# Softmax sums inverted in one folded reciprocal, and both parts of the mixer's weight chunks made on VectorE

## The chip, the core and the metric

The kernel runs on one core of a Trainium2 chip. The core has TensorE (matrix products, out of two weight buffers), VectorE and ScalarE (elementwise work, both can read the products' memory PSUM), GpSimd (elementwise work on the local memory SBUF alone), SyncE (here only a queue that issues transfers) and 16 DMA engines. Each engine runs its own list of instructions in order, and they meet at semaphores. The metric is the device time of one execution in microseconds; lower is better.

## The reference, cut to what matters

Two layers, each a mixer and a feed-forward part, over 16 meta tokens and 512 tokens of width 1024, in float32. The mixer has three branches of 8 heads: attention with forget decay (FOX), latent attention (MLA) and sliding-window attention (SWA).

```python
for l in range(DEPTH):
    h = mixer_block(h, ...)      # h + (sum of 3 gated branches) @ w_o
    h = conv_ffn(h, ...)         # h + (silu(gate) * val) @ w_down, after a convolution of width 3

# in each branch, for each head:
p = jax.nn.softmax(s, axis=-1)
out = jnp.einsum('bhqk,bkhd->bqhd', p, v)
```

The softmax is made without its division: the product of the exponentials with the values is divided by the exponentials' sums at the end, as a product with the inverted sums.

## The kernel before

**Products in three parts.** Every float32 weight block is split: `wh` is its high part (rounded to the format in which TensorE is fast), `wl` what is left. The activations are split alike (`xh`, `xl`), and a product is `wh*xh + wh*xl + wl*xh`. One block is 128x128 weights against 528 columns in two halves: six matmuls, lines 1357, 1360, 1362 in `gemm`.

**Weight chunks.** A layer has 1080 blocks in the order of `PLAN`: 488 of the mixer, then 64 of `w_o`, 352 of the up projection and 176 of the down projection. Eight blocks are one chunk of 128x1024, 135 chunks a layer. SP loads a chunk into one of two places of `raw` (`load`, line 734). VectorE casts it into `wh` (`high_part`, line 1670), GpSimd subtracts and writes `wl` in four pieces (`chunk_low`, line 817). `wh` and `wl` have three places each. At block 8c of the order, VectorE casts chunk c + 2 and GpSimd makes its low part, and SP loads chunk c + 4, once the low part of chunk c + 2 has let its place go.

**The mixer's order.** `mixer_plan` writes one list of events. Each event has an index, which is a block's number, and a rank; each engine's list is the same events sorted by index and rank, some of them moved by a table `LAG`. Between its blocks TensorE so finds the small products of the attention.

**Jobs.** A job is two heads of one branch: jobs 0 to 3 are FOX, 4 to 7 SWA, 8 to 11 MLA. Job j begins with its scores at block `BEGIN[j]` = 65, 94, 122, 161, 192, 222, 250, 282, 319, 354, 384, 429. Its steps:

- `M`, `MM` (from 25 blocks ahead): scores whose row maxima VectorE takes (lines 1962 and 1940), and `NT`: TensorE transposes the maxima (line 1509) and ScalarE places them as the shift.
- `STM`, `ST`: transposed scores (lines 1540 to 1546), VectorE adds the mask (1972, 1985), ScalarE takes the exponential (1255, 1258 for the meta tokens, 1272, 1274).
- `PVM`, `PV`: the products with the values (1565, 1588), two blocks behind the scores. The sums of the exponentials come from columns of ones in the same products.
- `O`: ScalarE copies heads to `oraw` and sums to `osum` (line 1011). `PVM`'s copies into the same tiles wait until GpSimd has read `oraw` of the job before.
- `recip`: VectorE inverts `osum` in four pieces of 128x132, one a block, from block `BEGIN[j]` + 15 (line 1993). Each head's sum stands 64 times, once in each of its 64 partitions.
- `heads`: VectorE multiplies `oraw` by `osum` (line 1998), four blocks later and lagged by two. `head copy`: ScalarE casts it into `oth`, GpSimd writes `otl` (line 1001). The branch's output blocks `y` take these.

**Norms.** A projected tile is normed through its statistic: TensorE sums squares (line 1376), VectorE adds (1797), ScalarE guesses the root (1028 to 1030), VectorE makes one Newton step (`newton`, 1686 or 1688, then 1691) and multiplies (1887 and others). A query tile `mq` of the latent branch is multiplied with the rotation first (1830, 1832 into `rawt`), and its statistic waits for that.

## Time and profile before

| what | value |
|---|---|
| median of 3 runs | 1982.04 us (1978.26 to 1982.62) |
| span of the profiled execution, first to last instruction | 1979.4 us |
| mean granted clock of TensorE | 0.995 |
| TensorE busy | 1914.7 us, 97% |
| VectorE busy | 1159.0 us, 59% |
| ScalarE busy | 766.2 us, 39% |
| GpSimd busy | 1025.5 us, 52% |
| DMA traffic | 156.30 MB, mean 79 GB/s |

The profiled execution has no time of its own beside its span. The span is 1979.4 us and the runs' median 1982.04 us, so some 2.6 us lie around it.

A matmul's end is modelled and overlaps its neighbours, so busy TensorE time does not say how fast it is, but a wait of TensorE shows as idle time with what released it. The first layer's mixer lies at 0 to 545 us, the second's at 1000 to 1540 us; `w_o` and the feed-forward part follow each.

### The profile page before, as it was taken

The numbers are of one execution on the slowest core, as the hardware profiler recorded it, in microseconds if no ns is written. First come the engines' busy times: TensorE is split into PE (matmuls) and PEld (weight loads), VectorE is DVE, ScalarE is ACT, GpSimd is POOL, SyncE is SP. The second block draws the span as 40 slices with busy tenths as digits, with TensorE's granted clock in tenths as the row PEclk, the third lists the DMA queues.
The fourth block names the chain that finished last, engine by engine and source line by source line (L and its number), as shares of the span: only waits on it lengthen the run. The fifth ranks groups of instructions, "written<-read, shape, count | busy, mean of one in ns | idle before, by whom it ended". The sixth has DMA issues, their size and how long they took to land.

```text
span 1979.4 us, 36478 instructions
## 1 busy us (share of the span) xinstructions
PE 1914.7 (97%) x14396; PEld 1817.1 (92%) x14396; DVE 1159.0 (59%) x2121; ACT 766.2 (39%) x1514; POOL 1025.5 (52%) x1306
## 2 busy tenths in 40 slices
PE   7899999999999999999998999999999999999999
PEld 7889998888999999999997899988889999999887
DVE  7665476787465666552256654767874655665411
ACT  5455666655223222220044556666553232222100
POOL 7655454544364444544477455544443645445553
PEclk9999999999999999999999999999999999999999
DMA  4212121211232322332332121112112423323332
GB/s 149 75 44 65 54 65 44 63 45 55 65 129 85 97 86 86 97 93 93 93 109 76 43 65 54 63 46 65 45 53 65 141 86 97 97 86 96 96 97 96
DMA packets 44802, 156.30 MB, mean 79 GB/s; under 512 B 5012, under 2 KB 5268, under 8 KB 44504
## 3 DMA queue, kind: packets, MB, share of 16 engines
q1 hardware_dynamic: 44488, 153.75, 24.7%
q8 instruction: 114, 1.87, 0.4%
q14 instruction: 56, 0.46, 0.1%
q10 hardware_dynamic: 144, 0.22, 0.0%
HBM read 149.63 MB, written 4.26 MB: 78 GB/s over the span
## 4 chain that ended last, share of the span: by engine, by line
PE 77%; DVE 12%; ACT 4%; issue 3%; POOL 2%; DMA 1%; SPq 0%; DVEq 0%; ACTq 0%; POOLq 0%
PE ps L1357 20%; PE ps L1360 19%; PE ps L1362 19%; PE ps L1588 5%; PE ps L1372 2%; PE ps L1368 2%; PE ps L1371 2%; PE ps L1376 2%; DVE osum L1993 1%; DVE rstd L1691 1%; PE ps L1540 1%; PE ps L1501 1%; POOL wl L817 1%; DVE ps L1962 1%; DVE square L1686 1%
## 5 line engine op out<-in xcount | busy, mean ns | idle before, releaser
L817 POOL TENSOR_TENSOR wl<-raw,wh 128x256 fp32r<-128x256 f32 x1076 | 798.7, 773 | 746.5 <-DVE wh L1670 739.9
L1357 PE MATMUL ps<-xh,wh 128*128 128x264 f32 (+1 forms) x2880 | 810.7, 303 | 12.5 <-DVE wl L1750 9.4
L1360 PE MATMUL ps<-xl,wh 128*128 128x264 f32 (+1 forms) x2880 | 764.3, 286 | 0.0
L1362 PE MATMUL ps<-xh,wl 128*128 128x264 f32 (+1 forms) x2880 | 585.4, 285 | 0.0
L1357 PEld LDWEIGHTS ps<-xh,wh 128*128 128x128 f32 x2880 | 546.7, 190 | 31.1 <-issue 18.3
L1360 PEld LDWEIGHTS ps<-xl,wh 128*128 128x128 f32 x2880 | 547.4, 190 | 17.0 <-issue 8.9
L1362 PEld LDWEIGHTS ps<-xh,wl 128*128 128x128 f32 x2880 | 451.2, 190 | 0.0
L1670 DVE CAST wh<-raw 128x1024 fp32r<-128x1024 f32 x270 | 206.6, 765 | 176.0 <-PE ps L1357 89.1
L1588 PE MATMUL ps<-pt,vx 128*128 128x512 f32 (+7 forms) x480 | 157.8, 409 | 3.9 <-ACT pt L1274 2.3
L1985 DVE TENSOR_TENSOR ps<-ps,cst 128x128 f32<-128x128 f32 (+6 forms) x240 | 74.8, 313 | 145.3 <-PE ps L1546 111.0
L1274 ACT ACTIVATE pt<-ps 128x256 f32<-128x256 f32 (+5 forms) x224 | 78.5, 363 | 112.5 <-DVE ps L1985 111.2
L1324 ACT ACTIVATE cv<-ps,prm 128x528 f32<-128x528 f32 (+1 forms) x44 | 34.6, 786 | 209.0 <-DVE ps L2039 209.0
L1357 PE MATMUL ps<-oth,wh 128*128 128x264 f32 (+1 forms) x384 | 111.5, 312 | 2.1 <-ACT ssum L1011 1.7
L2039 DVE TENSOR_TENSOR ps<-ps,rstd 128x528 f32<-128x528 f32 (+1 forms) x88 | 62.1, 706 | 80.5 <-PE ps L1362 80.4
L1360 PE MATMUL ps<-otl,wh 128*128 128x264 f32 (+1 forms) x384 | 100.9, 283 | 0.0
L1993 DVE RECIPROCAL osum<-osum 128x132 f32<-128x132 f32 x96 | 90.0, 958 | 13.2 <-ACT oraw L1011 13.0
L1360 PE MATMUL ps<-al,wh 128*128 128x264 f32 x352 | 93.1, 285 | 0.0
L1357 PE MATMUL ps<-ah,wh 128*128 128x264 f32 x352 | 93.0, 284 | 0.0
L1540 PE MATMUL ps<-xq,xk 97*17 97x16 f32 (+15 forms) x288 | 78.2, 290 | 8.8 <-ACT ptm L1255 4.0
L1501 PE MATMUL ps<-xk,xq 96*128 96x400 f32 (+13 forms) x256 | 71.6, 300 | 9.1 <-DVE nm L1962 3.0
L1588 PEld LDWEIGHTS ps<-pt,vx 128*128 128x128 f32 x480 | 74.6, 191 | 6.2 <-ACT pt L1274 4.1
L1001 POOL TENSOR_TENSOR otl<-oraw,oth 128x528 fp32r<-128x528 f32 x24 | 34.5, 1437 | 87.5 <-ACT oth L1011 86.7
(194 smaller groups left out, 3440.9 us busy)
## 6 DMA issues: line engine op xcount, KB each, us to landing
raw<-weights SPq DMA_DIRECT2D x270, 512.0 KB, 3.5
h<-tokens SPq DMA_DIRECT2D x4, 528.0 KB, 6.9
h<-tokens SPq DMA_DIRECT2D x8, 264.0 KB, 6.0
residual<-h SPq DMA_DIRECT2D x8, 264.0 KB, 5.0
h<-residual SPq DMA_DIRECT2D x8, 264.0 KB, 5.9
out<-h SPq DMA_DIRECT2D x8, 256.0 KB, 4.7
cst<-constants SPq DMA_DIRECT2D x1, 1048.0 KB
extra<-positions SPq DMA_DIRECT2D x18, 4.1 KB
```

Of the source, the lines that this page charges most:

```text
L817: ins = nc.gpsimd.tensor_tensor(wl[c % SPLIT][:, part], raw[:, c % RAW, part], wh[c % SPLIT][:, part].bitcast(F32), ALU.subtract)
L1274: ins = nc.scalar.activation(pt[0:nk, i, 0:nq], bank[0:nk, 0:nq], ACT.Exp)
L1357: a = nc.tensor.matmul(out, a_hi, x_hi[:, sl], start=first, stop=False)
L1360: nc.tensor.matmul(out, a_hi, x_lo[:, sl], start=False, stop=False)
L1362: ins = nc.tensor.matmul(out, a_lo, x_hi[:, sl], start=False, stop=last)
L1501: ins = nc.tensor.matmul(bank[:, col:col + nk], xq[rows, i, e, q], xk[rows, i, e, k0:k0 + nk], start=True, stop=True)
L1540: nc.tensor.matmul(out, xk[rows, i, e, keys], xq[rows, i, e, q], start=True, stop=False)
L1588: ins = nc.tensor.matmul(heads_out[:, c:c + nq], vals, pt[:, i, 0:nq], start=t == 0, stop=t == 4)
L1670: nc.vector.tensor_copy(wh[c % SPLIT][:, :], raw[:, c % RAW, :]).then_inc(s_hi, 1)
L1985: nc.vector.tensor_tensor(sc, sc, cst[0:nk, a:a + n], ALU.add).then_inc(scores_masked.sem, scores_masked.tick((l, j, e, t)))
L1993: nc.vector.reciprocal(osum[:, a:a + T // 4], osum[:, a:a + T // 4]).then_inc(dve_step.sem, dve_step.tick((l, "recip", j, q)))
L2039: nc.vector.tensor_tensor(src[:, skip:T], src[:, skip:T], rstd[:, skip:T], ALU.mult).then_inc(up_scaled.sem, up_scaled.tick((l, t)))
```

## The change

Part one, the inverted sums. In every job but 11 the four `recip` steps and their pieces are replaced:

- `fold` (block `BEGIN[j]` + 15): SP copies the two heads' sums, 2 x 528 numbers, out of one partition each, into 32 partitions of 33 (in rows 96 to 127 of the tile `krr`, two places taken in turn).
- `recip` (3 blocks later): VectorE inverts these 32x33 numbers in one instruction.
- `unfold` (same index): SP stores them to a tensor `inverse` in HBM; `spread` (7 blocks behind `fold`): SP loads each head's 528 inverted sums into its 64 partitions of `osum`, once the store is done.
- `heads` and `head copy` come 9 blocks later than before (`FOLD[2] - 4`).

Part two, the weight chunks. For the chunks of the mixer, from the fourth chunk of the program on, VectorE makes both parts: `high_part` as before, then `low_part`, one subtraction of 128x1024 right behind it. GpSimd makes none of them. For the feed-forward part nothing changes. The rest of the diff gives each part and engine a semaphore of its own, and code for sharing the work that these settings leave unused.

```diff
+FOLD = [3, 7, 13]
+FOLD_N = 2 * T // (P - MQ)
+UNFOLDED = [11]
...
-        for q in range(4):
-            put(i + q, 6, "recip", j, q)
+        if folded(j):
+            put(i, 2, "fold", j)
+            put(i + FOLD[0], 6, "recip", j, 0)
+            put(i + FOLD[0], 7, "unfold", j)
+            put(i + FOLD[1], 8, "spread", j)
+            i += FOLD[2] - 4
+        else:
...
+HIGH_AT = {"dve": 0, "act": 0, "pool": 0}
+LOW_AT = {"dve": 0, "pool": 0}
+POOL_PIECE = 256
+FIRST = 3
+MIX_HIGH, FFN_HIGH = "dve", "dve"
+MIX_DVE, FFN_DVE = 1024, 0
...
+def low_by(c):
+
+    d = CW if c == 0 else 0 if c < FIRST else MIX_DVE if in_mixer(c) else FFN_DVE
+    return {"dve": (0, d), "pool": (d, CW)}
...
             def load(n):
...
-                    sp.wait_ge(s_lo, n - RAW + 1)
+                    for sem, value in low_done(n - RAW):
+                        sp.wait_ge(sem, value)
...
+                    elif s[0] == "fold":
+                        j = s[1]
+                        sp.wait_ge(heads_copied.sem, heads_copied.at(l, j, 1))
+                        sp.wait_ge(meta_heads_copied.sem, meta_heads_copied.at(l, j))
+                        half_rows = (P - MQ) // 2
+                        for e in range(2):
+                            a = e * half_rows
+                            sp.dma_start(fold(j)[a:a + half_rows, :],
+                                         osum[e * HD:e * HD + 1, :].rearrange("o (r c) -> o r c", c=FOLD_N)).then_inc(
+                                sums_folded.sem, sums_folded.tick((l, j), 16))
+                    elif s[0] == "unfold":
+                        j = s[1]
+                        sp.wait_ge(dve_step.sem, dve_step.at(l, "recip", j, 0))
+                        sp.dma_start(inverse[l, j, :, :].rearrange("e (r c) -> (e r) c", c=FOLD_N), fold(j)).then_inc(
+                            inverse_stored.sem, inverse_stored.tick((l, j), 16))
+                    elif s[0] == "spread":
+                        j = s[1]
+                        sp.wait_ge(inverse_stored.sem, inverse_stored.at(l, j))
+                        for e in range(2):
+                            sp.dma_start(osum[e * HD:(e + 1) * HD, :],
+                                         inverse[l, j, e:e + 1, :].broadcast_to([HD, T])).then_inc(
+                                inverse_spread.sem, inverse_spread.tick((l, j), 16))
...
+            def low_part(c):
                 if c >= CHUNKS:
                     return
...
+                a, b = low_by(c)["dve"]
+                if b <= a:
+                    return
+                dve.wait_ge(*high_done(c))
+                nc.vector.tensor_tensor(wl[c % SPLIT][:, a:b], raw[:, c % RAW, a:b], wh[c % SPLIT][:, a:b].bitcast(F32),
+                                        ALU.subtract).then_inc(chunk_low["dve"].sem, chunk_low["dve"].tick((c,)))
...
                         j, q = s[1], s[2]
+                        if folded(j):
+                            dve.wait_ge(sums_folded.sem, sums_folded.at(l, j))
+                            nc.vector.reciprocal(fold(j), fold(j)).then_inc(
+                                dve_step.sem, dve_step.tick((l, "recip", j, 0)))
+                            continue
...
                         j = s[1]
-                        dve.wait_ge(dve_step.sem, dve_step.at(l, "recip", j, 3))
+                        if folded(j):
+                            dve.wait_ge(inverse_spread.sem, inverse_spread.at(l, j))
+                        else:
+                            dve.wait_ge(dve_step.sem, dve_step.at(l, "recip", j, 3))
                         nc.vector.tensor_tensor(oraw[:, :], oraw[:, :], osum[:, :], ALU.mult).then_inc(
                             heads_ready.sem, heads_ready.tick((l, j)))
```

VectorE's list of the kernel before, behind the scores of job 0: the row maxima of job 1 (`ISA` into `nm...`), the reciprocals of job 0, a chunk's CAST at block 80 (the first reciprocal stands right ahead of it).

```order
L1670 CAST wh_52<-raw 128x1024 [waits chunk_started,chunk_loaded0]
L1993 RECIPROCAL osum<-osum 128x132
L1797 SCALAR_TENSOR_TENSOR ssum<-teps,ps 128x528 [waits tile_scaled_down,statistic_ready]
L1962 ISA ps,nmx<-ps,cst 128x400 [waits scores_for_max]
L1962 ISA nmx 128x1
L1993 RECIPROCAL osum<-osum 128x132 x2
L1962 ISA ps,nmx<-ps,cst 128x272 [waits scores_for_max]
L1962 ISA nmx 128x1
L1686 TENSOR_TENSOR square<-ssum,square 128x528 [waits rsqrt_guess_ready]
L1691 SCALAR_TENSOR_TENSOR rstd<-square,rstd 128x528 [waits dve_step]
L1887 SCALAR_TENSOR_TENSOR q_87<-rawt,gain,rstd 128x528 [waits key_doubled,key_low_part,tile_normed]
L1998 TENSOR_TENSOR oraw<-oraw,osum 128x528 [waits dve_step]
```

The same place in the changed kernel:

```order
L1818 CAST wh_52<-raw 128x1024 [waits chunk_started,chunk_loaded0]
L1828 TENSOR_TENSOR wl_55<-raw,wh_52 128x1024 [waits chunk_high_part_by_dve]
L1955 SCALAR_TENSOR_TENSOR ssum<-teps,ps 128x528 [waits tile_scaled_down,statistic_ready]
L2120 ISA ps,nmx<-ps,cst 128x400 [waits scores_for_max]
L2120 ISA nmx 128x1
L2149 RECIPROCAL krr<-krr 32x33 [waits sums_folded]
L2120 ISA ps,nmx<-ps,cst 128x272 [waits scores_for_max]
L2120 ISA nmx 128x1
L1847 TENSOR_TENSOR square<-ssum,square 128x528 [waits rsqrt_guess_ready]
L1852 SCALAR_TENSOR_TENSOR rstd<-square,rstd 128x528 [waits dve_step]
L2045 SCALAR_TENSOR_TENSOR q_87<-rawt,gain,rstd 128x528 [waits key_doubled,key_low_part,tile_normed]
```

Four reciprocals and the product of the heads (`oraw`) are gone from here, one short reciprocal of `krr` and the subtraction into `wl` have come.

ScalarE's list of the kernel before, ahead of the scores of job 6, from the Newton guess to the shift's copies; `oth` is the high part of job 5's heads.

```order
L1028 ACTIVATE square<-ssum 128x528 [waits statistic_taken,tile_scaled_down]
L1029 ACTIVATE rstd<-square 128x528 [waits act_step]
L1030 ACTIVATE square<-rstd 128x528 [waits act_step]
L1011 ACTIVATE oth<-oraw 128x528 [waits heads_ready]
L1011 ACTIVATE xq<-ps 1x384 [waits shift_transposed]
L1011 ACTIVATE xq<-ps 1x128
```

In the changed kernel the same instruction stands between the exponentials of job 6:

```order
L1391 ACTIVATE ptm<-ps,prm 17x16 [waits meta_product_done,meta_scores_masked]
L1391 ACTIVATE ptm<-ps,prm 17x16
L1408 ACTIVATE pt<-ps,prm 128x512 [waits product_done,scores_masked]
L1410 ACTIVATE pt<-ps 128x256 [waits product_done,scores_masked]
L1129 ACTIVATE oth<-oraw 128x528 [waits heads_ready]
L1410 ACTIVATE pt<-ps 128x256 [waits product_done,scores_masked]
L1129 ACTIVATE oraw<-ps 64x16 [waits heads_low_part,meta_product_done]
L1129 ACTIVATE osum<-ps 64x16
```

`oth` now follows the second exponential (`pt`) of job 6. Behind the third stand the meta copies into `oraw` and `osum`, which wait for GpSimd's `otl` (`heads_low_part`).

## Rows read from the trace of the kernel before

**Rows 1.** Windows of the two mixers: stretch, length, busy us (instructions) of each engine, clock, DMA.
```profile
60.00:545.00 485.00, 464.68 (x3386) 429.46 (x3386) 315.12 (x696) 269.40 (x587) 242.82 (x284) 0.99 0.18 56
1060.00:1540.00 480.00, 459.23 (x3403) 424.47 (x3402) 311.30 (x678) 267.20 (x582) 243.25 (x285) 1.00 0.19 58
```
**Rows 2.** Waits of TensorE: who for whom, us in total, times, longest us.
```profile
PE ps L1376 <- DVE rawt L1832: 8.5, 9, 1.1
PE ps L1509 <- DVE nm L1940: 4.7, 5, 2.1
...
PE ps L1540 <- ACT ptm L1255: 4.0, 2, 2.0
```
**Rows 3.** Groups of the page: count, busy us, mean ns, idle before them.
```profile
L817 POOL TENSOR_TENSOR wl<-raw,wh 128x256 fp32r<-128x256 f32 x1076 | 798.7, 773 | 746.5 <-DVE wh L1670 739.9
...
L1670 DVE CAST wh<-raw 128x1024 fp32r<-128x1024 f32 x270 | 206.6, 765 | 176.0 <-PE ps L1357 89.1
...
L1993 DVE RECIPROCAL osum<-osum 128x132 f32<-128x132 f32 x96 | 90.0, 958 | 13.2 <-ACT oraw L1011 13.0
```
**Rows 4.** Timeline of VectorE ahead of job 1's shift: start us, us, what.
```profile
100.17 0.97 DVE L1993 RECIPROCAL osum<-osum 128x132 f32<-128x132 f32 x1
...
104.05 1.81 DVE L1993 RECIPROCAL osum<-osum 128x132 f32<-128x132 f32 x2
...
109.34 0.70 DVE L1998 TENSOR_TENSOR oraw<-oraw,osum 128x528 f32<-128x528 f32 x1
```
**Rows 5.** Timeline of TensorE at four waits, in brackets the idle time and its releaser.
```profile
111.22 0.33 PE L1509 MATMUL ps<-cst,nm 128*128 128x128 f32 x1 [2.08 <-DVE nm L1940]
...
299.95 0.39 PE L1540 MATMUL ps<-xq,xk 97*128 97x256 f32 x1 [1.97 <-ACT ptm L1255]
...
335.62 1.13 PE L1376 MATMUL ps<-sq,cst 96*128 96x264 f32 x4 [0.98 <-DVE rawt L1832]
...
460.69 1.13 PE L1376 MATMUL ps<-sq,cst 96*128 96x264 f32 x4 [1.08 <-DVE rawt L1832]
```
**Rows 6.** Timeline of VectorE ahead of the last three of these waits.
```profile
286.50 1.80 DVE L1993 RECIPROCAL osum<-osum 128x132 f32<-128x132 f32 x2
...
293.93 1.73 DVE L1691 SCALAR_TENSOR_TENSOR rstd<-square,rstd 128x528 f32<-128x528 f32 x1
...
333.34 0.68 DVE L1670 CAST wh<-raw 128x1024 fp32r<-128x1024 f32 x1
...
455.34 1.81 DVE L1993 RECIPROCAL osum<-osum 128x132 f32<-128x132 f32 x2
```
**Rows 7.** Line 1691, the Newton step: duration ns min/median/max.
```profile
L1691 DVE SCALAR_TENSOR_TENSOR rstd<-square,rstd x56: 707/709/1733, 35.0 to 1611.1; 128x528 f32<-128x528 f32 x56
```
**Rows 8.** Windows around three falls of the clock, columns as in rows 1.
```profile
110.00:120.00 10.00, 8.79 (x59) 8.59 (x60) 3.73 (x13) 7.54 (x20) 8.35 (x10) 0.83 0.00 1
296.00:310.00 14.00, 11.87 (x63) 10.11 (x62) 3.96 (x9) 9.27 (x22) 7.12 (x9) 0.76 0.15 46
...
1100.00:1110.00 10.00, 7.93 (x54) 7.55 (x53) 4.56 (x14) 6.49 (x17) 7.15 (x8) 0.83 0.01 2
```
**Rows 9.** Line 1750, VectorE's subtraction for the first chunk, columns as in rows 7.
```profile
L1750 DVE TENSOR_TENSOR wl<-raw,wh x1: 1226/1226/1226, 8.0 to 8.0; 128x1024 fp32r<-128x1024 f32 x1
```
**Rows 10.** Timeline of GpSimd beside the Newton step at 293.93.
```profile
293.48 1.62 POOL L1001 TENSOR_TENSOR otl<-oraw,oth 128x528 fp32r<-128x528 f32 x1
```
**Rows 11.** Chain that ended last, start of layer 1: start us, us, what.
```profile
1031.29 4.98 POOL wl L817 x4
```
**Rows 12.** Timeline of VectorE, start of layer 1.
```profile
1062.01 1.43 DVE L1670 CAST wh<-raw 128x1024 fp32r<-128x1024 f32 x1 [2.76 <-DMA raw<-weights]
```
**Rows 13.** Timeline of ScalarE, the second exponential of job 1.
```profile
118.96 0.51 ACT L1274 ACTIVATE pt<-ps 128x400 f32<-128x400 f32 x1 [0.54 <-DVE ps L1985]
```
**Rows 14.** Timeline of TensorE, the product that takes it.
```profile
121.79 0.83 PE L1588 MATMUL ps<-pt,vx 128*128 128x400 f32 x2
```
**Rows 15.** DMA issues: count, KB each, median us to landing.
```profile
raw<-weights SPq DMA_DIRECT2D x270, 512.0 KB, 3.5
```

## What I expected

> **What bounds the kernel now.** I read the windows of each engine's busy time first, because they split the span by stage. In the mixers TensorE is busy 464.68 of 485 us and 459.23 of 480 us [rows 1]; the feed-forward stages between them are not changed. So TensorE bounds the kernel, and a change to VectorE can give back only TensorE's waits in the mixers: 20 us a layer, and what the clock loses beside them. Next come the waits of TensorE, longest in total first [rows 2]: for the turned query tiles (`L1376` on rawt, nine times), for a job's maxima (`L1509`, where two of the five waits are of 2.1 us), and for the meta probabilities (`L1540` on `L1255`, two of 2.0 us). No row there has TensorE wait for GpSimd's low weight parts, so that these come sooner is worth nothing by itself. Then the costliest groups of the page [rows 3]: 1076 low parts on GpSimd (798.7 us), 270 CASTs on VectorE, 96 reciprocals of 0.96 us. Last, the timelines of the engines around each long wait of TensorE [rows 5, 6].
>
> **Reciprocals.** Each of 24 jobs has 4 x 0.958 us on VectorE [rows 3]. In 22 jobs one takes their place, of 33 elements a partition where each now has 132; by length it takes a quarter, 0.24 us. VectorE saves 22 x (3.83 - 0.24) = 79 us. What that is worth shows at two places, where the reciprocals stand in an unbroken run of VectorE's work that TensorE waits for.
> - At the transposed maxima of job 1 VectorE works almost without a pause from the first reciprocal at 100.17 to the last maximum, and TensorE, whose transpose begins at 111.22, waits 2.08 us for it [rows 4, 5]. In this run go four reciprocals (3.83) and the product at 109.34 (0.70); a subtraction (1.23) and the short reciprocal (0.24) come: 3.06 us less, more than the wait. Two layers: -4.2 us by the 2.1 of [rows 2].
> - At the start of job 6 TensorE waits 1.97 us for the meta probabilities [rows 5]. Before it VectorE has reciprocals (two of them, 1.80 us, at 286.50), then a Newton step of 1.73 us at 293.93 [rows 6] that takes 0.71 elsewhere [rows 7]. Four reciprocals go, less a subtraction at block 240: 2.4 us, more than the wait. Two layers: -4.0 us.
>
> **Clock.** Behind these waits the granted clock falls to the lower of its levels (1.2 of 2.4 GHz) for a while: 0.83 over 10 us, 0.76 over 14 us, 0.83 over 10 us [rows 8]. That is 10 x 0.17 + 14 x 0.24 + 10 x 0.17 = 6.8 us. If the waits go, it should stay up. But a wait that grows past 2 us (below) may bring new falls; I take -4.8, between 0 and -6.8.
>
> **Low parts on VectorE.** Blocks 0 to 487 of a layer are 61 chunks; less the first three of the program, 119 chunks get a subtraction of 128x1024 on VectorE. The one that is there now takes 1.226 us [rows 9]: +146 us. With the reciprocals VectorE has 67 us more on 626 busy of 965 [rows 1], about 72%. GpSimd loses 119 x 4 x 0.77 = 368 us in the mixers. That helps VectorE: the Newton step `L1691` runs from 0.707 to 1.733 us [rows 7], and the one of 1.73 has a head part of GpSimd beside it (1.62 us from 293.48) [rows 10]. Such slowing also touches the CAST (1.43 us at 1062.01, the mean is 0.765) [rows 3, 12]. The Trainium skill (GPSIMD Engine Reference, 1. Specifications) says that GpSimd's SBUF interfaces are shared with VectorE and contend with instructions of two SBUF inputs; the trace agrees with it. The same rule speaks against the change, as the subtraction has two SBUF inputs itself: GpSimd keeps some 118 us of work in 965, so 12% of the subtractions would be about 1 us longer, 14 us of VectorE's time, a tenth of which may reach TensorE; by the rule the sum is 1 us less of a gain, by the row of 1.226 alone it is as below.
>
> Where does 1.23 us at a chunk's start reach TensorE? CAST and subtraction follow each other, 1.9 us in one piece, and what stands behind them waits.
> - Query tiles. The second mq tile of a layer has its CAST at 333.34 right ahead of its two products, and TensorE already waits 0.98 us for these [rows 6, 5]: +1.23. One more mq tile stands so, three blocks ahead of its statistic; for the others reciprocals go just before (the last tile: 1.81 us of them at 455.34, a wait of 1.08 us [rows 6, 5], which I count as gone in both layers, -2). Cost: at most 4 x 1.23 = 4.9; I take +4.
> - Scores. 18 chunk starts a layer fall into the score phases, between mask, exponential and product. In the forget and window jobs there is room: the exponential that ended at 119.47 is used at 121.79, 2.3 us later [rows 13, 14]. The 7 chunk starts a layer in the four latent jobs are tight, as VectorE norms keys there: at most 14 x 1.23 = 17 us, at least 0. I take a quarter of that, nearest to the row with room: +4.
> - Other waits that stand behind reciprocals, under 1 us each: -1.
> - Start of layer 1. The chain of waits runs through GpSimd's low parts there (4.98 us for one chunk at 1031.29) [rows 11], and VectorE waits 2.76 us for a weight load that they hold back [rows 12]. Both go, and the CAST behind is 0.7 longer than the mean: at most 3.5 us; VectorE gets its subtractions in exchange. I take -2. Start of layer 0: three CASTs in VectorE's unbroken run get a subtraction, 3.7 at most, shorter neighbours in exchange: +1.
>
> **Transfers and the later heads.** Per folded job SP issues two small loads, a store and two spreads; the chunk loads behind them in SP's order are needed 16 blocks later, so this costs nothing unless SP stands for over 8 us. The trace prints no landing for a small transfer; 0 and the 3.5 us of a 512 KB load [rows 15] bound it. The new reciprocal stands where the fourth stood, which begins 4.8 us behind the first (the row at 104.05 holds two) [rows 4]; without three of them (2.9) and with a subtraction (1.23) 3.1 us are left. So VectorE waits at most 0.4 us a job there, 9 us in all, mostly off TensorE's path. The product of the heads moves 9 blocks later and in jobs 0, 1, 4, 5 and 9 lands among the next job's scores. Behind it ScalarE's copy, GpSimd's 1.62 us [rows 10] and ScalarE's meta copies follow. In the 2.3 us of room this mostly fits: +1 for both.
>
> **Sum:** -4.2 - 4.0 - 4.8 - 2 - 1 - 2 = -18; +4 + 4 + 1 + 1 = +10; together -8 us. The span of 1979.4 us lies 2.6 us under the median of the runs, 1982.04, and its ends are not changed. Forecast: 1974 us.
>
> **Rivals.**
> 1. VectorE is too full at chunk starts: the tight terms take their upper bounds (scores +17, query tiles +5), the clock falls again behind the grown waits (clock term 0), and the rest stays: -4.2 - 4.0 - 2 - 1 - 2 + 22 + 2 = +11, 1993 us. It decides from the point where more than half of the 14 latent chunk starts show in TensorE's waits. For it: VectorE is at 72% and works in order, its masks are on the shortest loop. Against it: the room of 2.3 us [rows 13, 14], and GpSimd's slowing of VectorE goes.
> 2. The late heads: ScalarE stands at the copy behind the product (0.70), copies (about 0.65), then stands at the meta copies for GpSimd's 1.62, 3.0 us in all. Ten places x (3.0 - 2.3) is 7 us with the room, 30 us without: 1981 to 2004, taken as 1983. For it: they stand between two exponentials in ScalarE's order. Against: the room.
> 3. The transfers are slower than the chunk load bounds them, as two in series behind a load of weights: 7 us instead of 3.5 puts VectorE to wait 3.9 us x 22 = 86 us, as long as the reciprocals were. Then only GpSimd's relief is left, and the subtractions cost what they cost: 1983 us. The Trainium skill (DMA: Bandwidth & Descriptors, Anatomy of one DMA) has about 2.0 us fixed for one DMA on GpSimd's path; by it the fold fits in the 3.1 us, and this rival falls. No row here shows a small landing.
> 4. Larger gain: nearly all of the mixers' waits behind VectorE go, and the clock stays up: the 18, 2 more from the clock, and a third (10) of the 30 us that are left of the 41 of gaps [rows 1], less costs of 5: -25, 1957 us. For it: GpSimd's relief speeds every Newton chain, which I gave no term of its own.
>
> **Chances.** Forecast 0.52 (own range 1966 to 1980), rival 4 0.18, rival 1 0.13, rival 2 0.09, rival 3 0.08. What can be told from no change is 0.2%, 4 us: 1978 to 1986. The forecast's own range is below 1978 in five parts of six: 0.44, rival 4 gives 0.18, rivals 2 and 3 0.04: faster 0.66. Same: 0.08 of the forecast, 0.01 of rival 1, 0.04 and 0.05 of 2 and 3: 0.18. Slower: 0.12 of rival 1, 0.04 of 2 and 3: 0.16. Range 1960 to 1986.
>
> **What would show it.** Right: the waits of 2.1 us at `nm` and 2.0 us at `ptm` are gone, and the granted clock is 1.00 in those stretches; the wait at the second mq tile is about 2.2 us; GpSimd is busy some 370 us less, VectorE some 40 to 70 us more; the CAST's mean is near 0.69 us. Wrong: waits of the products for exponentials in the latent jobs over 8 us in all (rival 1), of ScalarE for GpSimd's head parts that TensorE's waits repeat (rival 2), of VectorE at the folded reciprocal over 1 us each (rival 3). The feed-forward windows must stay as they are; if they move, the sum was made on the wrong stage.

## The result, and the profile after

The changed kernel takes 2019.96 us (median of 4 runs, 2018.09 to 2021.79) against 1981.61 us before (4 runs, 1978.26 to 1982.62). The ratio is 1.0198, 95% interval 1.0184 to 1.0213: 38 us slower. I had forecast 1974 us and a range of 1960 to 1986; the result lies far outside it, on the other side of no change. Every time here is of fast executions: one of the four of run e1 took 3072 us at a mean granted clock of 0.557 and is left out.

Windows of the profiled execution after, by stage (stretch, length, busy us and instructions of each engine, clock, DMA):

```profile
60.00:553.00 493.00, 459.94 (x3302) 421.56 (x3301) 334.57 (x707) 265.12 (x581) 98.35 (x77) 0.99 0.20 60
553.00:1018.00 465.00, 464.93 (x3805) 464.54 (x3804) 242.32 (x339) 97.27 (x140) 214.40 (x298) 1.00 0.30 95
1080.00:1580.00 500.00, 469.01 (x3427) 430.93 (x3427) 340.25 (x700) 267.92 (x582) 97.29 (x77) 0.99 0.20 61
```

Beside [rows 1]: the feed-forward stage is full as it was. In the mixers TensorE now misses 33 and 31 us of these stretches, where it missed 20 and 21. GpSimd is relieved as meant (98 us for 243). The first product of `w_o` starts at 588.1 us instead of 569.6, and the last one of layer 1's `w_o` 36.9 us late: 18.5 us are lost in each mixer. The loss is not spread evenly: TensorE's statistic product (`L1376` before, `L1524` after) that began at 206.84 us begins at 206.62 now, so nothing is lost up to there; the one of 311.88 comes 2.9 us late, the one of 477.87 17.9 us late. Most of it falls into the part where the latent branch's tiles are made and its jobs run.

The waits of TensorE after, beside [rows 2] (for whom: us in total, times, longest):

```profile
PE ps L1524 <- DVE rawt L1990: 16.2, 10, 3.2
...
PE ps L1649 <- DVE nma L2120: 7.0, 4, 3.4
PE ps L1657 <- DVE nm L2098: 6.8, 7, 1.8
PE ps L1649 <- DVE nmx L2120: 4.7, 10, 1.0
...
PE ps L1688 <- ACT ptm L1391: 4.4, 6, 1.4
```

The query tiles' wait (`L1524`, before `L1376`) has doubled from 8.5 us. The maxima's waits (`nm`, `nma`, `nmx` at `L1649`, before `L1501`, and `L1657`, before `L1509`) have grown in number; the waits of 2.1 and 2.0 us that I meant to remove are no longer the longest of their kind, but many others are there.

The groups and transfers that answer to [rows 3, 9, 15], and the Newton step of [rows 7]:

```profile
L933 POOL TENSOR_TENSOR wl<-raw,wh 128x256 fp32r<-128x256 f32 x600 | 434.5, 756 | 453.6 <-DVE wh L1818 453.1
...
L1818 DVE CAST wh<-raw 128x1024 fp32r<-128x1024 f32 x270 | 204.1, 756 | 178.6 <-PE ps L1505 101.1
L1828 DVE TENSOR_TENSOR wl<-raw,wh 128x1024 fp32r<-128x1024 f32 x120 | 171.7, 1431 | 4.1
...
L1828 DVE TENSOR_TENSOR wl<-raw,wh x120: 1224/1226/2295, 8.0 to 1578.4; 128x1024 fp32r<-128x1024 f32 x120
...
osum<-inverse SPq DMA_DIRECT2D x44, 132.0 KB, 2.9
```

```profile
L1852 DVE SCALAR_TENSOR_TENSOR rstd<-square,rstd x56: 707/708/711, 35.5 to 1648.1; 128x528 f32<-128x528 f32 x56
```

The Newton step is never slowed now (1.733 us at worst before). But the subtraction, which I took at 1.226 us, has a mean of 1.431: most take 1.226, and 31 of the 120 take 1.52 to 2.30, each with a GpSimd instruction beside it. The CAST, which I expected at a mean of 0.69 us, has 0.756 (0.765 before).

At the two waits that were to go, and at the last query tile (the two of 1.97 us and 1.08 us in [rows 5] are the second and the third here), TensorE has now:

```profile
112.36 0.33 PE L1657 MATMUL ps<-cst,nm 128*128 128x128 f32 x1 [0.38 <-DVE nm L2098]
...
303.92 0.39 PE L1688 MATMUL ps<-xq,xk 97*128 97x256 f32 x1 [1.27 <-ACT ptm L1391]
...
477.73 1.13 PE L1524 MATMUL ps<-sq,cst 96*128 96x264 f32 x4 [3.23 <-DVE rawt L1990]
```

Ahead of the last of them VectorE stood for the fold's transfer, with the query tile's products behind:

```profile
475.77 0.36 DVE L2149 RECIPROCAL krr<-krr 32x33 f32<-32x33 f32 x1 [3.13 <-DMA krr<-osum]
```

The clock, 1.00 around the same product before (453 to 473 us there), falls behind this wait (columns of the windows above):

```profile
470.00:490.00 20.00, 16.77 (x122) 16.12 (x120) 15.91 (x34) 10.82 (x19) 3.98 (x3) 0.91 0.22 67
```

The loss to the subtractions shows best at the second query tile of the latent branch. VectorE's timeline there, then GpSimd's, then TensorE's:

```profile
336.33 0.68 DVE L1818 CAST wh<-raw 128x1024 fp32r<-128x1024 f32 x1
337.04 2.29 DVE L1828 TENSOR_TENSOR wl<-raw,wh 128x1024 fp32r<-128x1024 f32 x1
339.36 0.71 DVE L1988 TENSOR_TENSOR rawt<-ps,gq 32x528 f32<-32x528 f32 x1
340.08 0.70 DVE L1990 TENSOR_TENSOR rawt<-ps,gq 96x528 f32<-96x528 f32 x1
```

```profile
336.92 1.33 POOL L1101 TENSOR_TENSOR yq<-q,xq 96x528 fp32r<-96x528 f32 x1 [11.50 <-ACT xq L1129]
```

```profile
340.93 1.13 PE L1524 MATMUL ps<-sq,cst 96*128 96x264 f32 x4 [2.92 <-DVE rawt L1990]
```

Before, this wait was 0.98 us [rows 5]. The tile is ready ahead of this CAST (its last weight product begins at 335.60 us and takes 0.41); its first two products on VectorE stand behind 3.0 us of weight work, 1.06 us of which is what this subtraction takes over its usual 1.226, with GpSimd at work beside it.

The maxima of job 0 stand behind a chunk's start in the same way. VectorE, then TensorE:

```profile
62.46 1.23 DVE L1828 TENSOR_TENSOR wl<-raw,wh 128x1024 fp32r<-128x1024 f32 x1
63.60 0.70 DVE L1955 SCALAR_TENSOR_TENSOR ssum<-teps,ps 128x528 f32<-128x528 f32 x1
64.22 0.43 DVE L2120 CUSTOM_DVE_ANT_0 ps<-ps,cst 128x264 f32<-128x264 f32 x1
```

```profile
64.76 0.39 PE L1649 MATMUL ps<-xk,xq 66*128 66x272 f32 x1 [3.02 <-DVE nma L2120]
```

In k1 below, where nothing but the subtractions and SP's order differs, TensorE waits 1.47 us there.

### The profile page after: what moved, and what is told of

It reads as the page before. It is cut to its first block, busy times and chain, and to the rows that moved or that the text cites. A ratio compares the mean times of both kernels' runs of the same rounds, so it can differ in the third digit from the quotient of the medians.

```text
span 2016.3 us, 36044 instructions
## 1 busy us (share of the span) xinstructions
PE 1925.9 (96%) x14396; PEld 1821.9 (90%) x14396; DVE 1226.9 (61%) x2174; ACT 767.9 (38%) x1514; POOL 687.5 (34%) x830
## 3 DMA queue, kind: packets, MB, share of 16 engines
q8 instruction: 114, 1.87, 0.4%
## 4 chain that ended last, share of the span: by engine, by line
PE 73%; DVE 15%; issue 5%; ACT 5%; DMA 1%; SPq 0%; POOL 0%; DVEq 0%; ACTq 0%
PE ps L1505 19%; PE ps L1508 19%; PE ps L1510 18%; PE ps L1736 5%; DVE wh L1818 3%; DVE wl L1828 2%; PE ps L1520 2%; PE ps L1516 2%; PE ps L1519 2%; PE ps L1524 2%; PE ps L1649 1%; DVE rstd L1852 1%; PE ps L1688 1%; DVE ps L2143 1%; ACT square L1146 1%
## 5 line engine op out<-in xcount | busy, mean ns | idle before, releaser
L933 POOL TENSOR_TENSOR wl<-raw,wh 128x256 fp32r<-128x256 f32 x600 | 434.5, 756 | 453.6 <-DVE wh L1818 453.1
L1828 DVE TENSOR_TENSOR wl<-raw,wh 128x1024 fp32r<-128x1024 f32 x120 | 171.7, 1431 | 4.1
L1061 POOL TENSOR_TENSOR yq<-q,xq 64x528 fp32r<-64x528 f32 x32 | 51.6, 1613 | 172.0 <-ACT xq L1129 169.4
L1119 POOL TENSOR_TENSOR otl<-oraw,oth 128x528 fp32r<-128x528 f32 x24 | 36.9, 1537 | 177.7 <-ACT oth L1129 177.7
L1649 PE MATMUL ps<-xk,xq 96*128 96x400 f32 (+13 forms) x256 | 73.6, 308 | 19.0 <-DVE nma L2120 7.0
```

What stands on the lines that cost most here:

```text
L933: ins = nc.gpsimd.tensor_tensor(wl[c % SPLIT][:, part], raw[:, c % RAW, part], wh[c % SPLIT][:, part].bitcast(F32), ALU.subtract)
L1649: ins = nc.tensor.matmul(bank[:, col:col + nk], xq[rows, i, e, q], xk[rows, i, e, k0:k0 + nk], start=True, stop=True)
L1828: nc.vector.tensor_tensor(wl[c % SPLIT][:, a:b], raw[:, c % RAW, a:b], wh[c % SPLIT][:, a:b].bitcast(F32), ALU.subtract).then_inc(chunk_lo ...
```

## The experiments

All times are medians, each ratio is to the kernel before in the same group of runs, with its 95% interval.

| run | fold | low parts | chunk loads by SP | us | ratio |
|---|---|---|---|---|---|
| changed kernel | yes | VectorE, block 0 | block 0 | 2019.96 | 1.0198 [1.0184, 1.0213] |
| e1 | yes | GpSimd | block 0 | 1995.05 | 1.0072 [1.0055, 1.0089] |
| e2 | no | VectorE, block 0 | block 0 | 2054.39 | 1.0365 [1.0340, 1.0391] |
| e4 | yes | VectorE, block 3 | block 0 | 1995.16 | 1.0068 [1.0053, 1.0083] |
| e5 | yes | VectorE, quarters in blocks 0 to 3 | block 0 | 2033.51 | 1.0266 [1.0247, 1.0285] |
| f1 | yes, reciprocal 2 later | GpSimd | block 0 | 2014.12 | 1.0166 [1.0152, 1.0179] |
| f2 | no, heads 9 later | GpSimd | block 0 | 1983.05 | 1.0012 [1.0003, 1.0020] |
| f3 | as f1 | VectorE, block 3 | block 0 | 2011.95 | 1.0154 [1.0140, 1.0168] |
| f4 | as f1 | VectorE, block 5 | block 0 | 2089.29 | 1.0545 [1.0526, 1.0564] |
| f5 | no | VectorE, block 3 | block 0 | 2008.23 | 1.0142 [1.0126, 1.0157] |
| h1 | yes | GpSimd | block 5 | 1978.23 | 0.9989 [0.9980, 0.9998] |
| h2 | yes | VectorE, block 3 | block 5 | 1987.85 | 1.0032 [1.0019, 1.0045] |
| h4 | no | GpSimd | block 5 | 1986.62 | 1.0026 [1.0015, 1.0037] |
| k1 | yes | GpSimd | 5, from block 72 | 1971.51 | 0.9950 [0.9937, 0.9962] |
| k2 | yes | VectorE, block 3 | 5, from block 72 | 1974.64 | 0.9959 [0.9947, 0.9972] |
| k3 | yes | VectorE, block 0 | 5, from block 72 | 2013.42 | 1.0159 [1.0145, 1.0173] |
| k4 | yes, heads 3 sooner | GpSimd | 5, from block 72 | 1966.65 | 0.9926 [0.9912, 0.9939] |
| l1 | yes | VectorE, block 3, CAST too | 5, from block 72 | 1994.77 | 1.0072 [1.0059, 1.0084] |
| l2 | as k4 | VectorE, block 3 | 5, from block 72 | 1966.42 | 0.9924 [0.9911, 0.9938] |

"Block n" is the place within a chunk of eight blocks. All diffs are against the changed kernel.

### The two parts apart: e1, e2

```diff
-MIX_DVE, FFN_DVE = 1024, 0
+MIX_DVE, FFN_DVE = 0, 0
```

> Part one alone: the sums are inverted folded, and GpSimd makes the mixer's low weight parts as before. Theory (the loss of 38 us is in part two, in VectorE's longer piece of work at each chunk's start): near the kernel before or a little under it, 1970 to 1984 us, and the wait of 2.1 us ahead of job 1's shift is gone. Rival (the later heads and their transfers cost it): 2000 us or more.

```diff
-UNFOLDED = [11]
+UNFOLDED = list(range(12))
```

> Part two alone: all 24 jobs keep their four reciprocals and the place of their heads, VectorE makes both weight parts. Theory (loss in part two): at least as slow as the changed kernel, 2018 to 2045 us, as the 79 us of reciprocals stand in the same queue of VectorE. Rival (the loss is in the fold and the late heads): under 1995 us.

Neither reading held whole: e1 lies between its two ranges and e2 9 us above the theory's. Part two is the larger loss: alone +73 us, on top of the fold +25 (1.0198 to 1.0072). But part one alone is not the gain that I had forecast either: +14 us. VectorE's waits for transfers in e1, and its timeline at the last query tile:

```profile
DVE krr L2149 <- DMA krr<-osum: 31.6, 12, 4.8
DVE oraw L2164 <- DMA osum<-inverse: 17.4, 7, 4.3
```

```profile
461.80 0.36 DVE L2149 RECIPROCAL krr<-krr 32x33 f32<-32x33 f32 x1 [3.29 <-DMA krr<-osum]
462.19 0.71 DVE L1988 TENSOR_TENSOR rawt<-ps,gq 32x528 f32<-32x528 f32 x1
```

and of GpSimd and of SP's queue ahead of it:

```profile
455.02 2.83 POOL L933 TENSOR_TENSOR wl<-raw,wh 128x256 fp32r<-128x256 f32 x4 [7.60 <-DVE wh L1818]
```

```profile
447.45 10.75 SPq L814 DMA_DIRECT2D raw<-weights  x2
458.30 1.18 SPq L845 DMA_DIRECT2D krr<-osum  x2
```

ScalarE had copied the sums and heads by 454.3. SP stood in front of a chunk load until GpSimd's low part was done at 457.85, issued 512 KB of weights, and only then the fold, at 458.30. It landed 3.5 us later; VectorE stood 3.29 us for it with the query tile behind, and TensorE 3.38 us at 463.76.

### The low part elsewhere in the chunk: e4, e5

```diff
-LOW_AT = {"dve": 0, "pool": 0}
+LOW_AT = {"dve": 3, "pool": 0}
```

> The changed kernel, but VectorE makes the low part three blocks (some 5.4 us) behind the CAST, so that its work at a chunk's start is two shorter pieces. Theory (the long unbroken piece of 1.9 to 3 us delays what stands behind it): a third to two thirds of the loss comes back, 1994 to 2008 us. Rival (VectorE has too much work in all, wherever it stands): within 5 us of 2020. Second rival (what hurts is which single step stands behind it, not the length): as much is lost at other steps, 2010 to 2025.

```diff
+DVE_PIECES = 4
...
-                if n % BLK == LOW_AT["dve"]:
-                    low_part(n // BLK + AHEAD)
+                if n % BLK < DVE_PIECES:
+                    low_part(n // BLK + AHEAD, n % BLK)
```

> The changed kernel, but VectorE makes the low part in four pieces of 128x256, one a block at blocks 0 to 3 of the chunk; total work of VectorE grows by some 0.06 us a piece. Theory (length of the piece): most of the loss comes back, 1985 to 2000 us, since no step is delayed by more than 0.3 to 0.6 us. Rival (total work): 2020 us or a few us more.

e4 gives 25 us back, as expected; with GpSimd making the low parts (e1) it is no less. e5 was meant to do more and is 13 us slower than the changed kernel. A piece is dearer than I took it for:

```profile
L1831 DVE TENSOR_TENSOR wl<-raw,wh x477: 402/420/1575, 8.0 to 1595.3; 128x256 fp32r<-128x256 f32 x158, 128x1024 fp32r<-128x1024 f32 x1
```

Four pieces of 0.42 us are 1.68 us where one of 1.226 did, and beside GpSimd they reach 1.58 us each. The group took 249.1 us instead of 171.7. A second thing differs: VectorE stood 44.6 us for the fold's transfers where it stood 14.9 in the changed kernel; but in e4 it stood 41.4 us for them. How the 13 us divide was not measured. e5 changed the amount of work and says nothing about the length of a piece; l1 below does.

### More room for the reciprocal, later heads: f1, f2, f3, f4

```diff
-FOLD = [3, 7, 13]
+FOLD = [5, 8, 13]
```

f1 (with GpSimd's low parts):

> Part one alone again (GpSimd makes the low parts), but the folded reciprocal comes five blocks behind the fold instead of three, and the spread eight instead of seven; the heads stay where part one has them. In the run of part one alone VectorE stood 31.6 us, 12 times, up to 4.8 us, for the sums' transfer, and the last query tile stood behind one such wait. Theory (that wait is what makes part one slower than the kernel before): VectorE's wait for krr falls under 10 us in all, TensorE's wait at the last query tile falls from 3.5 to about 1.2 us, and the time to 1982 to 1990 us. Rival (the late heads cost it): 1992 to 1998 us as before.

f2 (no fold, no low parts on VectorE):

```diff
             for q in range(4):
                 put(i + q, 6, "recip", j, q)
+            if j != 11:
+                i += FOLD[2] - 4
```

> No fold and no low parts on VectorE: the kernel before with one thing changed, the product of the heads and ScalarE's copy behind it come nine blocks later in every job but 11. Theory (late heads cost little, the transfers' wait costs): 1979 to 1986 us. Rival (late heads): 1990 us or more.

f3 and f4 (f1's `FOLD`, and `LOW_AT` of VectorE at 3 and at 5):

> Both parts, low part three blocks behind the CAST (1995 us without more) and the folded reciprocal five blocks behind the fold. Theory: the two repairs add up, as they touch different waits: 1980 to 1990 us. Rival (VectorE at this load has no room left for either): 1992 us or more.

> As the run before, but the low part five blocks behind the CAST, one block past the middle of a chunk. Theory (length of the unbroken piece): within 4 us of the run with three blocks. Rival (it is a matter of which single steps stand behind it, as all events of a query tile end at fixed blocks of the plan): differs by over 6 us, in either direction.

The rival in f2 falls: late heads alone cost 2.4 us. My repair in f1 made part one 19 us slower instead of faster. VectorE's waits in f1, and SP's queue and VectorE at job 7's heads:

```profile
DVE oraw L2164 <- DMA osum<-inverse: 47.4, 18, 5.9
...
DVE krr L2149 <- DMA krr<-osum: 1.9, 3, 0.9
```

```profile
379.97 0.34 SPq L814 DMA_DIRECT2D raw<-weights  x1
380.35 1.13 SPq L857 DMA_DIRECT2D osum<-inverse  x2
```

```profile
384.90 0.71 DVE L2164 TENSOR_TENSOR oraw<-oraw,osum 128x528 f32<-128x528 f32 x1 [5.36 <-DMA osum<-inverse]
```

The 49 us of waiting are all there, moved from `krr` to `oraw`: the spread now stood behind a chunk load, which again waited for a low part. There the same waiting costs more, as a job's last maxima stand behind the heads in VectorE's order: TensorE waits 15.2 us for `nm` at `L1657` instead of 4.8 in e1, 4.18 us of it at 387.15, right behind the product above. f3 shares this (36.8 us of VectorE's waiting at `oraw`, 14.7 of TensorE's for `nm`), so the two repairs did not add up: it is 2 us from f1. In f4 the low part comes five blocks into the chunk, SP stands for it longer still, and VectorE waits 82.5 + 17.9 us for the fold's transfers: VectorE waits for a transfer that stands in SP's order behind VectorE's own work. That f4 is so far off says nothing on the length of a piece.

### The chunk loads later in SP's order: h1, h2, h4, f5

```diff
             def advance(l, i):
                 n = l * LB + i
-                if n % BLK == 0:
+                if n % BLK == (LOAD_AT if in_mixer(n // BLK) else 0):
                     load(n // BLK + AHEAD + RAW)
```

with `LOAD_AT = 5`. h1:

> Part one alone (1996 us), but SP issues the mixer's chunk loads five blocks later in its order. As it was, SP stood at a chunk's start for GpSimd's low part, and the fold's or the spread's transfer came right behind a load of 512 KB, landing 3.5 us late; VectorE stood 49 us for the two kinds of transfer (31.6 + 17.4). Moving the reciprocal two blocks moved these 49 us from one wait to the other. Theory (the fold's transfers are held up in SP's queue): VectorE's two waits fall under 15 us together, and the time to 1966 to 1980 us. Rival (the transfers are slow by themselves, three in series): the waits stay over 35 us and the time near 1990 us.

h2:

> Both parts, low part three blocks behind the CAST (1995 us), with the same later place of the chunk loads in SP's order. Theory: as above, 1966 to 1984 us, at most 8 us over part one with later loads. Rival (VectorE's load of work with the low parts is what is left): 1990 us or more.

h4:

> The control: the kernel before's work (four reciprocals a job, GpSimd's low parts) with only the mixer's chunk loads five blocks later in SP's order. Every theory expects no change, 1978 to 1984 us, as a load is needed 11 blocks behind its new place; a gain here would be the load's and not the fold's.

f5 (loads as they were, no fold):

> Part two alone, without the fold, its low part three blocks behind the CAST instead of right behind it (2054 us). Theory (the low part at a chunk's start joins other work that stands there): half or more of the 73 us comes back, 1995 to 2020 us. Rival (VectorE's total of work): 2040 us or more.

h1's waits of VectorE for the fold's transfers fell from 49 to 7.6 us (6.1 for `oraw`, 1.5 for `krr`), and its time by 17 us (1.0072 to 0.9989). Most of their slowness was their place. The control h4 was not neutral, though: it lost 5 us, and the one wait of TensorE that grew is for `vt`, once a layer near block 50, where a load now stood behind SP's wait for `nd`:

```profile
PE ps L1613 <- DVE vt L1967: 10.6, 2, 5.3
```

(this row is h1's; h4 has 10.4, the kernel before 2.6). That wait is in h2's 1988 as well (16.0 us), which so missed its range. f5 shows part two without the fold: the place three blocks later gives 46 of its 73 us back.

### The same, from block 72 on: k1, k2, k3, k4

```diff
-                if n % BLK == 0:
+                late = in_mixer(n // BLK) and n // BLK * BLK % LB >= LOAD_FROM
+                if n % BLK == (LOAD_AT if late else 0):
                     load(n // BLK + AHEAD + RAW)
```

k1:

> Part one alone, with the chunk loads five blocks later in SP's order only from block 72 of a layer on. The control showed that the later place costs 5 us by itself: a wait of 5.3 us for vt once a layer near block 50, where a load then stands behind SP's wait for nd. Theory: that wait goes and nothing else changes: 1978 less 5 to 6, so 1970 to 1975 us, and part one is worth -8 us once its transfers are not held up. Rival (the later loads gave the fold its gain only by shifting work around that wait): 1976 us or more.

k2:

> Both parts, low part three blocks behind the CAST, chunk loads later from block 72 on. Theory (what is left of part two's cost are VectorE's 119 subtractions in a queue with some room): 1978 to 1984 us, 6 to 10 us over part one alone with the same loads. Rival (in the right place the subtractions are free, as GpSimd's relief pays for them): within 3 us of part one alone.

k3:

> The changed kernel itself (low part right behind the CAST), with nothing changed but the place of the chunk loads in SP's order, from block 72 on. Theory (in the changed kernel the low part's place at the chunk's start is the loss, since VectorE stood only 15 us for the fold's transfers there): 2010 to 2020 us. Rival (the fold's transfers behind SP's waits are the larger loss there too): 1995 us or less.

k4 (`FOLD = [3, 6, 10]`):

> As the first kernel of this group, but the spread six blocks behind the fold and the heads ten, instead of seven and thirteen. Late heads alone cost 2.4 us. Theory: within 3 us of the first kernel, at best 2.4 us less. Rival (the spread then lands too late): VectorE waits at oraw over 15 us in all, and the time is over 1976 us.

k1 settles part one: 0.50% faster than before, 10 us, once its transfers are not held up; k4 adds 5 with sooner heads, twice what I had allowed. (No run has these later loads without the fold, so a little of the 10 us may be theirs. h4 says it is little: its profiled execution spans 7.0 us more than that of the kernel before, and its wait for `vt`, which k1 is built to avoid, is 7.8 us longer.) k3 settles the changed kernel: with SP's order put right it still takes 2013 us, 42 more than k1, and the one difference to k1 is that VectorE makes the low parts at the chunk's start. k2 shows that three blocks further on they cost 2 to 3 us, and the intervals of k1 and k2 overlap. (Three blocks are some 3.5 us, by 569.6 us for the mixer's 488 blocks, and not the 5.4 that I wrote ahead of e4.) The same query tile in k2, VectorE and then TensorE:

```profile
326.13 0.68 DVE L1820 CAST wh<-raw 128x1024 fp32r<-128x1024 f32 x1
326.84 0.71 DVE L1990 TENSOR_TENSOR rawt<-ps,gq 32x528 f32<-32x528 f32 x1
327.56 0.70 DVE L1992 TENSOR_TENSOR rawt<-ps,gq 96x528 f32<-96x528 f32 x1
...
329.03 1.22 DVE L1830 TENSOR_TENSOR wl<-raw,wh 128x1024 fp32r<-128x1024 f32 x1
```

```profile
328.42 1.13 PE L1526 MATMUL ps<-sq,cst 96*128 96x264 f32 x4 [0.59 <-DVE rawt L1992]
```

The tile's steps go first, the subtraction falls into the room behind them (VectorE is idle 0.79 us right after it), and TensorE waits 0.59 us instead of 2.92.

### Length or place: l1, and all repairs together: l2

l1 is k2 with the CAST moved as well:

```diff
-                if n % BLK == HIGH_AT["dve"] and n >= BLK:
+                if n % BLK == (3 if in_mixer(n // BLK + AHEAD) else 0) and n >= BLK:
                     high_part(n // BLK + AHEAD)
```

> Both parts with the later chunk loads, and CAST and subtraction together in one unbroken piece again, but three blocks behind the chunk's start. Together at the start they gave 2013 us, apart (CAST at the start, subtraction at three) 1975 us. Theory (place: 41 of the 86 tiles of a layer's mixer end at a chunk's start, and their first steps on VectorE stand behind whatever is put there): within 6 us of 1975, so 1969 to 1981 us. Rival (length of the unbroken piece, 1.9 us against 0.7 and 1.2): 2000 us or more.

l2 is k2 with `FOLD = [3, 6, 10]`:

> Both parts, subtraction three blocks behind the CAST, later chunk loads, spread at six and heads at ten blocks: all repairs together. Theory (the sooner heads are worth the 5 us here that they were with part one alone): 1967 to 1972 us. Rival (VectorE's subtractions fill the room that the sooner heads need): 1974 us or more.

l1 lands between the two, and outside both ranges: 1995 us. Of the 39 us between k3 and k2, moving the unbroken piece gives 19 (17 by the ratios), and parting it, with the CAST back at the chunk's start, the other 20 (22). So neither the place nor the length is the whole. The second share is not the length alone: in l1 VectorE also stands 17.2 us for the fold's transfers, in k2 5.2.

What makes the chunk's start a bad place is not shown. My reading ahead of l1 was that 41 of the 86 tiles of a layer's mixer end there and their first steps on VectorE stand behind the piece. The count is right (a tile of a full product is eight blocks too), the order is not: in `mixer_plan` such a step has rank 0 and the block that brings the CAST rank 9, so it stands right ahead of the CAST. At block 160 of the changed kernel, where `merged` takes a gate's tile:

```profile
192.76 0.71 DVE L1980 SCALAR_TENSOR_TENSOR merged<-ps,hsum 128x528 f32<-128x528 f32 x1 [3.26 <-PE ps L1510]
193.38 0.73 DVE L1818 CAST wh<-raw 128x1024 fp32r<-128x1024 f32 x1
194.15 1.52 DVE L1828 TENSOR_TENSOR wl<-raw,wh 128x1024 fp32r<-128x1024 f32 x1
195.59 0.18 DVE L2130 TENSOR_TENSOR ps<-ps,cst 17x32 f32<-17x32 f32 x1
```

These tiles make the unbroken run longer by their 0.7 us; what is delayed are the masks, maxima and statistics behind it, and the query tiles that end a block or more into the chunk.

l2 is as fast as k4 (1966.4 and 1966.7 us): in this place the second part costs nothing, and it also gains nothing. Both beat the kernel before, by 15 us.

## Why the prediction was wrong, step by step

The loss of 38 us (39 by the ratio), from the ratios of the runs: part one with SP's order put right -10 us (k1); the subtractions at the chunk's start +41 (1.0159 of k3 to 0.9950 of k1); SP's order in the changed kernel +8 (1.0198 to 1.0159, the changed kernel was timed in another group of runs than k3).

- **Low parts on VectorE, the step that failed.** The terms "query tiles +4" and "scores +4" had as their measured counterpart +41. TensorE's listed waits, k3 beside k1: for `rawt` 11.6 against 5.6 us, so +6, near my +4. For exponentials 24 against 18, so +6, near my +4. But for maxima (`nm`, `nma`, `nmx`) 23 against 10, +13, and for these I had no term at all. That makes 25 us of waits. The clock stands at its half level for 30.6 us instead of 6.8, in eight falls instead of one; 12 us would be the price if TensorE had work for all of that time. It is an upper bound: k3's four executions have mean clocks from 0.992 to 0.996, which is 8 us by the same sum, and their times differ by 2 us. The rest of the 41 is not placed. I had found the right steps behind the reciprocals and looked only there; at the chunk starts I looked at two kinds of step and not at the maxima, which stand behind the same CAST (64.76 us above).
- **Its size.** 119 x 1.226 = 146 us was to be put on VectorE; it was 170. The 31 long ones all have GpSimd beside them (2.29 us at 337.04). The Trainium skill (GPSIMD Engine Reference, 1. Specifications) says that the interfaces shared by VectorE and GpSimd contend with instructions of two SBUF inputs, and I had counted 14 us by it and left them out of the sum. The trace agrees, and the size was 24 us and not 14. It should have been in the sum. In return GpSimd's relief was to make the CAST shorter, and its mean hardly moved.
- **Reciprocals.** Right in the main: 0.36 us each (I took 0.24), the wait at job 1's shift is 0.38 us at 112.36 instead of 2.08 [rows 5]. The one at job 6 I had gone; it is 1.27 us, as subtractions came where reciprocals left: k1, without them, has no such wait there (at 295.01 us), and k3, with them, 1.28 us (at 308.12). The one at the last query tile I had gone too; it grew to 3.23 us, behind 3.13 us of VectorE's waiting for the fold's transfer. The transfer has a part in the changed kernel's `rawt` waits for this reason: 16.2 us there, 11.6 in k3.
- **Transfers.** "The chunk loads behind them cost nothing" was true and beside the point. I asked who stands behind the fold, and not behind whom the fold stands. My 9 us in all were met by 9.4 us in the changed kernel, but by luck: my bound was 0.4 us a job, and these are eight waits of up to 3.1 us, while for the other jobs VectorE came late itself. In e1, with VectorE less busy, the same wait is 31.6 us. Rival 3 had this place and, as its reason, transfers in series; h1 shows that it was SP's order. The transfers by themselves are fast, 2.9 us for the spread on the page and 1.9 and 1.4 us (medians) for the fold and the store. The Trainium skill (DMA: Bandwidth & Descriptors, Anatomy of one DMA) has about 2.0 us fixed for one on GpSimd's path. These are on SyncE's queue, and the fold's 1.9 us is near that, the store's 1.4 under it; it had no say in the result.
- **Clock.** I had -4.8 us. The profiled execution of the changed kernel is at half for 28 us, that of the kernel before for 20: the waits moved, and the falls with them. The other three of the changed kernel have lower mean clocks still, 0.988 to 0.992.
- **Late heads.** +1 for them and the transfers; the heads alone are +2.4 us (f2), so the size was near.
- **Start of the layers.** I had +1 and -2. At 91 us TensorE is 2.5 us late; at the start of layer 1 nothing is gained either (18.4 us late at 1038 us, 19.2 at 1062).
- **Rival 1** was nearest in its mechanism, VectorE too full at the chunk starts, with chance 0.13 and 1993 us. But its sign did not come: from 320 to 565 and from 1338 to 1590 us, with the latent jobs inside, the products wait 5.9 us in all for exponentials, and I had put the sign at over 8; the maxima and query tiles are what grew. Its price was too low for the same reason: it took the upper bounds of the two kinds of step that I had priced, and knew no third.

## What to carry to other kernels

Work that is moved to an engine with room by its average share is paid at the places where it lands: list everything that stands right behind the new instruction in that engine's order, every kind of it. And try the same work a few steps further on before giving it up: these 119 subtractions cost 41 us right behind the CAST and 2 to 3 us three blocks later. A small transfer on a queue that also waits for something else costs what the wait ahead of it costs; read the queue's order upwards as well as downwards. One of the two parts of this change was good, and no single run of the whole could have said so.

## What the runs showed of the hardware that I had not expected

- Cutting one VectorE subtraction of 128x1024 (1.226 us) into four of 128x256 makes 4 x 0.42 = 1.68 us, 0.11 us more a piece.
- Beside a GpSimd instruction on SBUF the subtraction of 1.226 us takes up to 2.29 us, and the one of 0.42 up to 1.58. The CAST of the same chunk reads one tile and is not spared: 0.687 us as a rule, up to 1.87. The reciprocal of 32x33 took 0.358 to 0.363 us in all 22.
- A reciprocal of 33 elements a partition takes 0.36 us where one of 132 takes 0.96: a quarter of the length takes three eighths of the time.
